# TensorE multiplies tokens by the identity in its gaps ahead of attention and once in each attention head

## The reference

```
h    = rmsnorm(x) @ w_in                       # 256 x 1024 @ 1024 x ~1960
swa  : 8 heads, head 64, window 128, bias by distance, a sink per head
fox  : 4 heads, head 64, logits + (F[t] - F[s]), F = cumsum(log_sigmoid(f))
mla  : 4 heads, q and k through latents of 256 and 128, rope, q.k over 96
p    = softmax(logits);  o = p @ v             # per head, causal
x    = x + rmsnorm(rmsnorm(concat(o)) @ w_out)
```

## Time and profile before

| what | value |
|---|---|
| three runs | 1015.9, 1017.51, 1023.0 us (median 1017.51) |
| the profiled execution | 1019.81 us, its span 1018.0 us, mean granted clock 0.913 |
| PE busy | 902.0 us, 89% of the span |
| DVE, ACT busy | 489.2 us, 424.9 us |
| chain that ended last, by engine | PE 67%, ACT 9%, DVE 9%, issue 7%, DMA 5% |
| attention heads, first transposes of head 0 to last product | 98.5 to 165.8 us |

### The profile page before, as it was taken

The page is one execution under the profiler, slowest core; times in us unless marked ns, Lnnn a source line. Parts: engine busy times, 40 slices in busy tenths (PEclk is TensorE's granted clock), DMA queues, the critical chain, the costliest instruction groups (busy, mean ns, idle before and its releaser), DMA issues.

```text
span 1018.0 us, 13414 instructions
## 1 busy us (share of the span) xinstructions
PE 902.0 (89%) x4944; PEld 724.0 (71%) x4944; DVE 489.2 (48%) x599; ACT 424.9 (42%) x533; POOL 143.9 (14%) x128
## 2 busy tenths in 40 slices
PE   5976996959999999499999998789999999999966
PEld 4864775449999998368788873557777777777742
DVE  1004434135666666310201032438998887787742
ACT  2112214135454544212110011138788778778740
POOL 0000000012424243200200000002212211212100
PEclk9997555979999999689699999699999999999998
DMA  9872000214545454213134344018999999999923
GB/s 373 293 195 93 0 1 0 98 69 169 203 170 202 168 203 169 79 62 145 42 131 158 131 159 165 1 65 337 352 358 359 348 360 361 350 358 358 352 86 121
DMA packets 29200, 194.54 MB, mean 191 GB/s; under 512 B 3736, under 2 KB 3992, under 8 KB 7536
## 3 DMA queue, kind: packets, MB, share of 16 engines
q1 hardware_dynamic: 25488, 182.56, 48.0%
q0 software_dynamic: 3680, 11.54, 4.0%
HBM read 183.07 MB, written 11.01 MB: 191 GB/s over the span
## 4 chain that ended last, share of the span: by engine, by line
PE 67%; ACT 9%; DVE 9%; issue 7%; DMA 5%; POOL 1%; ACTq 1%; DVEq 0%; POOLq 0%
PE psum L608 30%; PE psum L450 10%; PE psum L473 6%; ACT expert_w_high L373 5%; DMA line_scratch<-arena 4%; PE psum L458 3%; DVE expert_w_low L378 3%; PE psum L757 3%; PE psum L438 2%; ACT xw_high L921 2%; ACT junk L902 1%; PE psum L793 1%; ACTq L1074 1%; PE psum L550 1%; PE psum L580 1%
## 5 line engine op out<-in xcount | busy, mean ns | idle before, releaser
L378 DVE TENSOR_TENSOR expert_w_low<-ring,expert_w_high 128x2048 fp32r<-128x2048 f32 x64 | 158.0, 2471 | 49.3 <-ACT expert_w_high L373 49.2
L373 ACT ACTIVATE expert_w_high<-ring 128x2048 fp32r<-128x2048 f32 x64 | 121.7, 1904 | 31.2 <-DVE HT L1522 31.2
L450 PE MATMUL psum<-HT,ring 128*128 128x256 f32 x592 | 131.5, 384 | 0.0
L450 PEld LDWEIGHTS psum<-HT,ring 128*128 128x128 f32 x592 | 113.5, 193 | 17.2 <-issue 1.6
L378 DVE TENSOR_TENSOR ffn_w_low<-ring,ffn_w_high 128x2048 fp32r<-128x2048 f32 x33 | 80.2, 2432 | 68.1 <-ACT ffn_w_high L373 68.1
L921 ACT ACTIVATE arena<-psum 64x1024 f32<-64x1024 f32 (+5 forms) x50 | 41.1, 835 | 144.3 <-PE psum L608 43.4
L608 PE MATMUL psum<-ht_high,ffn_w_high 128*128 128x256 f32 x352 | 100.1, 284 | 1.1 <-DVE ffn_w_low L378 1.1
L608 PE MATMUL psum<-ht_low,ffn_w_high 128*128 128x256 f32 x352 | 99.8, 283 | 0.0
L608 PE MATMUL psum<-ht_high,ffn_w_low 128*128 128x256 f32 x352 | 99.7, 283 | 0.0
L373 ACT ACTIVATE ffn_w_high<-ring 128x2048 fp32r<-128x2048 f32 x33 | 63.1, 1915 | 86.9 <-PE psum L608 86.7
L608 PE MATMUL psum<-expert_w_high,xw_high 128*64 128x256 f32 x264 | 75.1, 284 | 4.9 <-issue 3.1
(11 more groups left out here) (281 smaller groups left out, 1559.9 us busy)
## 6 DMA issues: line engine op xcount, KB each, us to landing
ring<-units_in SPq DMA_DIRECT2D x165, 1024.0 KB, 5.1
results_scratch<-arena POOLq DMA_DIRECT2D x32, 256.0 KB, 4.0
const<-const_in SPq DMA_DIRECT2D x1, 2112.0 KB, 13.9
arena<-results_scratch SPq DMA_DIRECT2D x4, 512.0 KB, 5.2
rows<-rows_in SPq DMA_DIRECT2D x1, 1688.0 KB, 23.9
line_scratch<-arena POOLq DMA_DIRECT2D x1, 1536.0 KB, 36.5
small<-small_in SPq DMA_DIRECT2D x1, 1236.0 KB, 16.5
X<-x_in SPq DMA_DIRECT2D x1, 1024.0 KB, 4.8
```

The costliest lines, as they stand in the source:

```text
L373: nc.scalar.activation(parts_slot(n)[0], w, ACT.Copy).then_inc(hi_ready, 1)
L378: nc.vector.tensor_tensor(l, ring[:, n % RING, :], h.bitcast(fp32), SUB).then_inc(lo_ready, 1)
L450: last = mm(psum[:, bank, half * S:half * S + S], w[:, k * stride + half * P:k * stride + half * P + P], HT[:, k, :], start=k == 0, stop=k ...
```

## The change

`stay_busy` moves to the top of PE's program and takes a bank and a width. It now multiplies the identity by `HT`, the transposed normed tokens, which stay unchanged from the projection until after attention. PE calls it at four new places: 7 matmuls of 512 columns ahead of the wait for the normed latents, 3 of 512 after the up-projections, 2 of 512 after the waits for the query and key copies and so ahead of the first logits, and 1 of 256 in each of the 16 head turns, between the logits of head h+2 and the wait for `pt_sb`. The first call follows a new wait, `evac_dve` at 1, for DVE's copy out of bank 0. The two calls in the router keep their counts and bank; they read `HT` instead of `HN`. No other engine's program changes.

```
+            busy_with = HT[:, :, :].rearrange("p a b -> p (a b)")
+
+            def stay_busy(count, bank=0, n=512):
+
+                for _ in range(count):
+                    mm(psum[:, bank, 0:n], ident, busy_with[:, 0:n], start=True, stop=True)
+
...
+            pe.wait_ge(evac_dve, 1)
+            stay_busy(7)
             pe.wait_ge(lat_hn, 1)
...
             last.then_inc(lat_up, 1)
+            stay_busy(3)
             pe.wait_ge(qk_rot, 1)
...
             pe.wait_ge(kmt_sb, 1)
+            stay_busy(2)
...
                 if h + 2 < HEADS:
                     logits(h + 2)
+                stay_busy(1, n=256)
                 pe.wait_ge(pt_sb, h + 1)
...
-            def stay_busy(count):
-
-                for _ in range(count):
-                    mm(psum[:, 7, :], ident, HN[:, 0, 0:512], start=True, stop=True)
-
-            stay_busy(2)
+            stay_busy(2, 7)
...
-            stay_busy(3)
+            stay_busy(3, 7)
```

## The result

The change makes no gain: 1024.24 us in the median of 20 runs (1019.78 to 1030.13) against 1021.2 of 20 runs of before (1015.9 to 1023.0). The ratio is 1.0035 with a 95% interval of 1.002 to 1.0051, some 3.6 us slower. The forecast was 992, so it was wrong in direction and in size. The second rival, a clock that falls at the first head, stood at 1022 and has the right time within 2 us; both numbers were built on 1017.51, the median of three runs of before, 3.7 us under that of the twenty. The profiled execution took 1024.27 us, span 1022.5, mean granted clock 0.921 against 0.913.

The account below looks back on a forecast made before the run. The prediction took the heads to be bound by PE at half its clock. Lead-in 1.9 us plus heads 24.8 made 26.7 saved: 993.1 from the profiled execution, 990.8 from the median, taken as 992, own range 988 to 997, overall 987 to 1023.

Parts of the forecast that it names:

- second rival: Clock falls at the first head; added matmuls cost 0.86 us in ten turns, +4.6 us, 1022; chance 0.24.
- forecast's 24.8: Head turns at the full clock: 8.3 us saved in sliding-window, 12.5 in forget, 4.0 in latent turns.
- Steps 1 to 3: Lead-in calls of 7, 3 and 2 matmuls ahead of the heads: -1.8 - 1.8 + 1.7 = -1.9 us.
- Step 4: One 256-column matmul per head turn, clock full: turns of 2.3, 4.0 and 2.1 us, 24.8 us saved.
- step 3: Two matmuls ahead of the first logits, behind the waits, so not hidden: +1.7 us, clock full as heads begin.
- prices at the low clock: In head turns at 0.50, each added 256-column matmul costs 0.86 us.
- prices at the full clock: Head turns at 1.00 with the added matmul: 2.3 us sliding-window, 4.0 forget, 2.1 latent.
- first rival: Clock falls in the forget turns, whose matmuls mostly use 4 rows; 12.8 us saved, 1005; chance 0.18.
- slow rival: Clock never comes up in the heads, latent turns stay at 0.50; +11 to +13 us, 1029; chance 0.11.
- two rules of the Trainium skill: Transposes don't raise the clock; a continuously busy TensorE gets its full clock. The prediction's trace disagreed with both.

Follow-up runs that it names:

- rows: Kernel before, no added matmuls, every logits matmul over all 128 rows by zero-padded copies and tiles; 989.24 us, ratio 0.9701.
- lead: The change without the matmul in the head turns, only the 7, 3 and 2 ahead of the heads; 1019.36 us, ratio 0.9977 to before.
- rows_two: rows plus the calls of 7 ahead of the latents and 3 after the up-projections; 984.52 us, ratio 0.9648 to before.
- rows_change: rows plus the whole change, its 7, 3, 2 and one matmul per head turn; 988.89 us, ratio 0.9692 to before.
- rows_swa: Kernel before with full 128-row logits for the sliding-window heads alone, no added matmuls; 1006.83 us, ratio 0.986.
- fill: The change plus two 512-column identity matmuls in the rest at the first head, after the logits of head 1; 1006.54 us, ratio 0.9863 to before.
- fill_fox_rows: fill_only plus full 128-row logits for the forget heads alone; 989.10 us, ratio 0.9694 to before.
- fill_only: fill without the matmul in the head turns, so calls of 7, 3, 2 and 2; 1007.59 us, ratio 0.9867 to before.
- copies_only: Control for rows: same zeroing and key copies, but each logits matmul on its own 64, 4 or 96 rows; 1020.85 us, ratio 1.0009 to before.
- heads: The change without the three lead-in calls, only the 256-column matmul in each head turn; 1024.34 us, ratio 1.0037 to before.

## Why the prediction was wrong

**What bounds the kernel** was read rightly: PE at half its clock. rows has its clock at 1.00 through the heads and is 31 us faster, some 3 us of that by shorter turns on full rows. The forecast's 24.8 for the turns at a full clock, with 0.43 us paid in each, is not out of line with it; no run had 64- and 4-row turns at 1.00 throughout.

**Steps 1 to 3, the lead-in.** The sum of -1.9 us held, but not in the profile of the changed kernel. The start of the latents' transposes moves between executions (76.74 us there, 78.75 in lead, with the same program up to that point), so I measure from it to the first transposes of the probabilities. Before takes 20.58 us, rows 20.78. With the calls of 7 and 3, in rows_two, it is 17.25, and so 3.5 less than in rows (3.6 forecast); with the third call too, in rows_change, 18.96, so that call costs 1.7, as forecast. In the changed kernel it is 20.46: only 0.1 us gained. There the full clock did last to the latents' transposes, but it fell at 78.3, and the first four up-projection records took 2.86 us at 0.50; in lead they took 1.56, and the stretch 19.16. In rows_swa, which has none of the calls, they took 1.56 as well. Where the clock stands in the lead-in shifts between executions by about as much as this term is worth.

**Step 4 failed, in its condition "clock full".** The forecast put the chance at 0.47 because the fall at 98.5 "had two rests behind it and one is filled". None was. The prediction says itself in step 3 that the two calls stand behind the waits; so the rest of 1.42 us only moved ahead of them (92.08 in the timeline), and the rest of 1.67 us at the first head was not touched. Lead and the changed kernel both lose the clock there, and fill, which adds only a cover for the second rest, keeps it. The prediction listed just this fall as its second rival and gave it half the weight, with the same slip ("replaces only the first of two rests"). What spoke for that rival in the profile, that 64-row logits stand on both sides of the rest and had never raised the clock in 22 us, was there to be weighed.

**The prices at the low clock** held. A sliding-window turn took 4.54 us (3.69 + 0.86 = 4.55 forecast), a forget turn 7.98 (7.99). The latent turns came back earlier: the first took 2.98 us instead of 3.95, then 2.04, against 2.1 forecast. The second rival summed to +4.6 us; measured are +3.6. In the profile the lead-in gave 0.1 us (1.9 in the rival), turns 0 to 5 cost 3.7 (5.2; the first, 3.18 us long, began at the full clock), the forget turns 3.4 (3.4), and the rest gave back 3.3 (2.1).

**The prices at the full clock**, where fill shows them: 2.43 us for a sliding-window turn (2.3 forecast). Without the call they are 2.00, and on full rows 1.87, the loop of transposes, copy and product of the earlier trace rows. On full rows PE is no longer the bound (busy 11.19 of 11.90 us), so these 0.13 us are less than what 64-row logits cost it: at 0.50, where PE is the bound, a turn was 0.55 us shorter on full rows.

**The first rival** was right in its mechanism, once the rest is filled: the clock falls in the first forget turn, and fill_fox_rows shows that the rows are why. The slow rival did not occur in the changed kernel. Its mechanism, latent turns that stay at 0.50, did in lead, fill_only and rows_swa, whose turns have no added matmul and so are shorter rather than longer.

**The two rules of the Trainium skill** ("TensorE: Matmul & The Clock Gate", Part 4 and "Why this matters for your kernels"). That keeping TensorE busy gives its full clock is refuted by copies_only against rows: PE busy 22.12 of 22.20 us at 0.50 in one, 11.19 of 11.90 at 1.00 in the other. That transposes don't count had spoken for the slow rival; the rise behind nothing but transposes had spoken against it. The runs are divided: heads, rows and copies_only show that rise again, as the 16 transposes end, but in rows_swa the same 16 (89.5 to 93.1) left the clock at 0.50, and it stayed there until 101.8. So transposes alone can be followed by the full clock, but need not be.

What stays open is why the clock came back at 161.9 in before and at about the same place in copies_only, behind four latent turns on 96 rows, and not in lead, fill_only or rows_swa, whose latent turns have the same logits matmuls. Open too is what in fill's cover keeps the clock, the end of the rest or the 128-row work; no run covers the rest with thin work.

## What to carry to other kernels

Where a stretch is bound by TensorE and its granted clock is 0.50 although it never rests, look at the rows that its matmuls contract over before adding matmuls: full rows, zero-padded, cost no column and gave 31 us, where identity matmuls gave 14 at best and cost 3.6 as first placed. An added matmul belongs where TensorE waits; in a stretch that TensorE bounds it is pure cost unless the clock follows, which a look at the granted clock of that stretch tells at once. And a short rest at the seam of two stages can decide what comes behind it: covering 1.67 us was worth 17 us (fill against the changed kernel).

## What the hardware showed that I had not expected

The granted clock follows the rows in use and not only busy time: the same logits matmuls of 128 and 256 columns ran at 0.50 on 64, 4 and 96 rows and at 1.00 on 128 rows (copies_only and rows). Rows that multiply by zeros count as well. At one and the same clock, too, a turn is longer on fewer rows, 3.69 us on 64 rows and 3.14 on 128 at 0.50. A full clock is easier kept than got: 64-row turns held 1.00 for 12.3 us in fill_only but never brought it back from 0.50 (22.2 us in copies_only, and 24.05 us in the changed kernel even with a 128-row matmul of 256 columns in each turn). The forget turns, on 64, 4 and 4 rows, lost the clock within the first of them (fill, fill_only, rows_swa) and did not raise it in 28.4 us (before). Latent turns on 96 rows held it (8.2 us in fill_fox_rows).
